# The two seams of the expert stage rewritten: token rows scaled on VectorE, no softmax division, the last expert's rows in two halves, and the last layer norm by sum and square

## The reference

```python
# m = W_o(sum of three gated branches of x); one projection w_in feeds all branches
h = layer_norm(ALPHA * x + m, ln1_g, ln1_b)
# moe_ffn(h)
logits = jnp.dot(t, router_w) + router_b          # t: 520 tokens x 1024
probs = jax.nn.softmax(logits, axis=-1)           # 16 experts in 4 groups of 4
top_v, top_i = lax.top_k(probs.reshape(-1, 4, 4), 2)
best = jnp.argmax(jnp.sum(top_v, axis=-1), axis=-1)      # the best group
weights = sel_v / jnp.sum(sel_v, axis=-1, keepdims=True) # its two experts
for e in range(16):
    u = jax.nn.silu(t @ w_gate[e]) * (t @ w_up[e])       # 1024 -> 512
    out = out + gates[:, e:e + 1] * (u @ w_down[e])      # 512 -> 1024
y = layer_norm(ALPHA * h + out, ln2_g, ln2_b)
```

## Time and profile before

| | |
|---|---|
| median of 3 runs | 1061.76 us (1060.02 to 1062.53) |
| the profiled execution | 1062.88 us |
| its span in the trace | 1060.7 us |
| TensorE busy | 993.2 us, 94% |
| VectorE busy | 805.2 us, 76% |
| ScalarE busy | 472.1 us, 45% |
| GpSimd busy | 360.5 us, 34% |
| TensorE's mean granted clock | 0.974 of full speed |
| DMA traffic | 189.91 MB, 179 GB/s over the span |

### The profile page before, as it was taken

One profiled execution on the slowest core, in us unless ns is written; L12 is line 12 of the kernel. 1 busy time (PEld: TensorE's weight loads), 2 busy tenths in 40 slices (PEclk: granted clock), 3 DMA queues, 4 the chain that ended last, 5 costly groups with the idle time before them and its releaser, 6 DMA issues.

```text
span 1060.7 us, 19425 instructions
## 1 busy us (share of the span) xinstructions
PE 993.2 (94%) x7186; PEld 898.5 (85%) x7186; DVE 805.2 (76%) x993; ACT 472.1 (45%) x657; POOL 360.5 (34%) x268
## 2 busy tenths in 40 slices
PE   7999999999999999999999999986999999999940
PEld 7999999999999998999999999964677777777630
DVE  1498889888899985754345596255998989899968
ACT  4232322323222244234342323254887878787820
POOL 2444434444545761454444544401200000000050
PEclk9999999999999999999999999997999999999975
DMA  7332332323322231333335525377999999999562
GB/s 223 106 100 84 94 96 82 99 83 95 96 83 80 79 100 29 122 94 94 88 95 161 176 79 208 111 287 277 313 390 378 393 380 393 381 389 335 178 211 101
DMA packets 162376, 189.91 MB, mean 179 GB/s; under 512 B 5876, under 2 KB 113396, under 8 KB 162317
## 3 DMA queue, kind: packets, MB, share of 16 engines
q1 hardware_dynamic: 155819, 177.46, 49.4%
q0 software_dynamic: 3008, 10.55, 3.1%
q10 hardware_dynamic: 3505, 1.36, 0.5%
HBM read 178.57 MB, written 11.76 MB: 179 GB/s over the span
## 4 chain that ended last, share of the span: by engine, by line
PE 52%; issue 27%; POOL 13%; DVE 3%; DMA 2%; ACT 2%; POOLq 0%; DVEq 0%; ACTq 0%
PE pr L926 27%; PE pr L1099 14%; POOL w_lo L552 12%; PE work L1099 7%; DMA hs<-h_rows,ids 2%; PE work L1085 1%; POOL y_a L609 1%; PE work L1009 1%; DVE stats L1658 1%; DVE y_a L1656 1%; ACT h_f L780 1%; DVE y_b L1665 1%; PE work L1060 1%; DMA y_b<-y_rows,slot_b 0%; PE pr L1116 0%
## 5 line engine op out<-in xcount | busy, mean ns | idle before, releaser
L552 POOL TENSOR_TENSOR w_lo<-raw,w_hi 128x512 fp32r<-128x512 f32 x208 | 297.7, 1452 | 337.1 <-ACT w_hi L637 337.1
L926 PE MATMUL pr<-x_hi,w_hi 128*128 128x260 f32 x1264 | 254.9, 283 | 0.2 <-POOL w_lo L552 0.2
L926 PE MATMUL pr<-x_hi,w_lo 128*128 128x260 f32 x1264 | 254.8, 283 | 0.0
L926 PE MATMUL pr<-x_lo,w_hi 128*128 128x260 f32 x1264 | 254.3, 283 | 0.0
L641 ACT ACTIVATE ev<-pr 128x520 f32<-128x520 f32 x96 | 58.1, 605 | 376.2 <-PE pr L926 376.2
L926 PEld LDWEIGHTS pr<-x_hi,w_hi 128*128 128x128 f32 x1264 | 194.9, 188 | 0.6 <-POOL w_lo L552 0.4
L926 PEld LDWEIGHTS pr<-x_hi,w_lo 128*128 128x128 f32 x1264 | 194.9, 188 | 0.0
L926 PEld LDWEIGHTS pr<-x_lo,w_hi 128*128 128x128 f32 x1264 | 194.3, 188 | 0.0
L1258 DVE SCALAR_TENSOR_TENSOR work<-b_pad,par,work 128x512 f32<-128x512 f32 x224 | 148.1, 743 | 0.0
L637 ACT ACTIVATE w_hi<-raw 128x512 fp32r<-128x512 f32 x208 | 118.9, 623 | 3.5 <-issue 2.2
L588 POOL DMA_INDIRECT hs<-h_rows,ids x16 | 20.1, 1259 | 256.2 <-DVE ids L1518 215.9
(11 more groups left out here) (290 smaller groups left out, 1693.6 us busy)
## 6 DMA issues: line engine op xcount, KB each, us to landing
raw<-in_w_in_dram SPq DMA_DIRECT2D x80, 512.0 KB, 3.7
w_gate<-in_expert_w_gate_dram SPq DMA_DIRECT2D x16, 2048.0 KB, 14.2
w_up<-in_expert_w_up_dram SPq DMA_DIRECT2D x16, 2048.0 KB, 14.3
w_down<-in_expert_w_down_dram SPq DMA_DIRECT2D x16, 2048.0 KB, 12.8
y_rows<-y_out SPq DMA_DIRECT2D x16, 384.0 KB, 12.2
raw<-in_w_a_out_dram SPq DMA_DIRECT2D x8, 512.0 KB, 3.6
raw<-in_w_c_out_dram SPq DMA_DIRECT2D x8, 512.0 KB, 3.6
raw<-in_w_b_out_dram SPq DMA_DIRECT2D x8, 512.0 KB, 3.7
```

Source lines behind the costliest of these rows:

```text
L552: pool.tensor_tensor(w_lo[:, slot, k], raw[:, slot, k], w_hi[:, slot, k].bitcast(F32), ALU.subtract).then_inc(w_split, 1)
L926: mm = pe.matmul(pr[slot][:, h, 0:HALF], w[:, slot, k, :], x[:, k, h * HALF:(h + 1) * HALF], start=(k == 0 and w is w_hi and x is hi), sto ...
```

## The change

- **Seam in.** The gain of the first norm is multiplied into m by ScalarE right behind each projection (zg_ready), so that the router's weights are not scaled. h_f, diag, its matmuls and h_affine are gone. TensorE transposes m itself, the five blocks between the logits' blocks, and VectorE writes the token rows from PSUM: reciprocal deviation times row, plus the bias row (b_row), which SP loads. SP stores the rows ahead of expert 2's gate and up loads.
- **Router.** Exp's table is loaded by a dummy activation behind the roots. The division by the softmax sum is left out (the weights are renormalised later, and the choice doesn't change with the scale). The second top search and the search over the groups run interleaved (behind waits for all but the newest of VectorE's instructions), and the multiplication of the one-hots by the best group moves to pick_weights.
- **First expert.** keep_busy puts 20 transposes of the identity in front of the first turn and 12 behind it. The first gate product starts on hs_hi alone; in its first chunk the low part of the tokens comes last (lo_waits).
- **Slots.** One find_slots for both experts of a token, after expert 13; order_slots after expert 14.
- **Samples.** The 8 sample tokens are spread over all 128 partitions, 16 partitions a token and 64 elements each (CS = 64): TensorE spreads their slots and weights by one matmul, GpSimd fetches with row numbers of 64 elements, and their mean and variance are summed over partitions by two matmuls with block_mean. Two new constant matrices are made by GpSimd. The gain and bias rows for them come by 16 small DMAs.
- **Last expert.** down_last finishes one half of the columns, then the other. ScalarE copies each half into a buffer of its own (y_last), and issues its store itself. GpSimd waits for these two and the other stores, without SP between. The rows of the second norm are loaded by load_back, ahead of the store of expert 14.
- **Second norm.** summed_up sums the row by accum_out and makes the negative mean; ScalarE squares the centred row with accum_out and takes the root. The samples are handled between blocks 2 and 3.

The semaphores are renamed and regrouped to match. The core of the diff, with the constant matrices, the renamed semaphores and the branch for further passes left out:

```diff
-        sp.dma_start(h_back[0:TS, 4, :], h_rows[TP:T, :]).then_inc(back_in, 16)
...
+        sp.dma_start(sh_back, h_rows[TP:T, :].rearrange("s (c f) -> (s c) f", f=CS)).then_inc(back_in, 16)
+        for i, row in enumerate((ln2_g, ln2_b)):
+            sp.dma_start(ln2_rows[:, i, :], row[0].partition_broadcast(P)).then_inc(ln_in, 16)
+            for s in range(TS):
+                k = P // TS
+                sp.dma_start(sln2[s * k:(s + 1) * k, i, :], row[0].rearrange("(c f) -> c f", f=CS)).then_inc(ln_in, 16)
...
+    sp.dma_start(b_row[:], ln1_b[0].partition_broadcast(P)).then_inc(b_row_in, 16)
...
+    h_out()
     expert_load(first, 2, TURN[2], "gate")
     expert_load(first, 2, TURN[2], "up")
...
+    def fetch_samples(dst, which, landed, table):
+
+        pool.indirect_dma_start(out=dst, out_offset=None, in_=table.rearrange("r (c f) -> (r c) f", f=CS),
+                                in_offset=bass.IndirectOffsetOnAxis(ap=s_idx[:, which:which + 1], axis=0)).then_inc(landed[4], 16)
...
     fetch(y_a, slot_early, y_a_in, y_rows[0:EARLY * C, :])
+    pool.wait_ge(sample_dve, 2)
+    fetch_samples(sy_a, 0, y_a_in, y_rows[0:EARLY * C, :])
...
+        pool.wait_ge(first.stored, 16 * E)
+        pool.wait_ge(first.half_stored, 32)
         fetch(y_b, slot_b, y_b_in, y_rows[0:E * C, :])
+        fetch_samples(sy_b, 2, y_b_in, y_rows[0:E * C, :])
...
+        act.wait_ge(sq_ready, i + 1)
+        act.activation(m[:, i, :], m[:, i, :], ACT.Copy, scale=par[:, i * NROWS + R_L1G:i * NROWS + R_L1G + 1]).then_inc(zg_ready, 1)
...
+    act.wait_ge(tok_std, 2)
+    act.activation(agg[0:1, 0, 1:2], eps_t[0:1, 0:1], ACT.Exp)
+    act.wait_ge(var_logits_mm, 2)
...
+    def last_rows_out(ps, t, q, row0):
+        x = E - 1
+        for h in range(2):
+            cols = slice(h * D // 2, (h + 1) * D // 2)
+            act.wait_ge(ps.done["down"], t * CH + CH + 2 * (h + 1))
+            act.activation(y_last[:, cols], work[0][0:C, h, :], ACT.Copy).then_inc(ps.half_ready, 1)
+            act.wait_ge(ps.half_ready, q * 2 + (h + 1))
+            act.dma_start(y_rows[bass.ds(x * C + row0, C), cols], y_last[:, cols]).then_inc(ps.half_stored, 16)
...
+    def deviation(b):
...
         act.wait_ge(var_ready, b + 1)
...
+        act.activation(pr[0][:], y_a[:, b, :].rearrange("p (h n) -> p h n", h=2), ACT.Square, bias=agg[:, s, 1:2],
+                       accum_out=agg[:, s, 2:3]).then_inc(std2_ready, 1)
+        act.wait_ge(std2_ready, 2 * b + 1)
+        act.activation(agg[:, s, 3:4], agg[:, s, 2:3], ACT.Sqrt, scale=1.0 / D, bias=eps_t[:, 1:2]).then_inc(std2_ready, 1)
...
+    def turn_rows(b):
+        n = P if b < 4 else TS
+        work_wait(pe, f"ht{b}")
+        for k in range(KB):
+            mm = pe.transpose(work[TILE[f"ht{b}"]][0:n, k // 4, k % 4 * P:(k % 4 + 1) * P], m[:, k, b * P:b * P + n], ident[:])
...
+    mm.then_inc(var_logits_mm, 1)
+    pe.wait_ge(zg_ready, KB)
+    turn_rows(0)
+    turn_rows(1)
     logits((2, 3))
...
+    turn_rows(2)
+    logits((4,))
+    turn_rows(3)
+    turn_rows(4)
+    logits((5, 6, 7)).then_inc(var_logits_mm, 1)
...
+    def keep_busy(n):
+
+        for _ in range(n):
+            pe.transpose(pr[0][:, 1, 0:P], ident[:], ident[:])
...
+            if lo_waits and i == 0:
+                for kk in range(k_of):
+                    cols = slice(kk * 512, (kk + 1) * 512)
+                    pe.matmul(out(0), hi[:, kk, :], w_hi_i[:, cols], start=(kk == 0), stop=False)
+                    pe.matmul(out(0), hi[:, kk, :], w_lo_i[:, cols], start=False, stop=False)
+                pe.wait_ge(ps.hs_lo_ready, t + 1)
+                for kk in range(k_of):
+                    mm = pe.matmul(out(0), lo[:, kk, :], w_hi_i[:, kk * 512:(kk + 1) * 512], start=False, stop=False)
+                mm.then_inc(ps.done[kind], 1)
+                continue
...
-        product(ps, "down", 0, t, u_hi_last, u_lo_last, lambda h: work[0][0:C, h, :], 2, last=True)
+        for h in range(2):
+            for k in range(CH):
+                if h == 0:
+                    pe.wait_ge(ps.lo_dve["down"], t * CH + (k + 1))
+                cols = slice(h * 512, (h + 1) * 512)
+                w_lo_k, w_hi_k = chunk("down", 0, k, w_e_lo), rounded("down", k, True)
+                for x, w in ((u_hi_last, w_hi_k), (u_hi_last, w_lo_k), (u_lo_last, w_hi_k)):
+                    mm = pe.matmul(work[0][0:C, h, :], x[:, k, :], w[:, cols], start=(k == 0 and x is u_hi_last and w is w_hi_k),
+                                   stop=(k == CH - 1 and x is u_lo_last))
+            mm.then_inc(ps.done["down"], 2)
...
+        if ps is first:
+            keep_busy(20)
         turn(ps, n0)
+        if ps is first:
+            keep_busy(12)
...
+            if m:
+                pe.wait_ge(ps.hs_lo_ready, t + 1)
+            else:
+                pe.wait_ge(ps.hs_hi_ready, t + 1)
...
+        if ps is first:
+            pe.wait_ge(const_ready, 6)
+            pe.wait_ge(sample_dve, 1)
+            pe.matmul(pr[1][:, 1, 8:13], spread[:], s_own[:], start=True, stop=True).then_inc(sample_mm, 1)
...
+        dve.wait_ge(round_done, DONE[f"ht{b}"])
+        dve.scalar_tensor_tensor(h_tok[b][:].rearrange("p (h t) -> p h t", h=2), work[TILE[f"ht{b}"]][0:n], r_tok[0:n, b:b + 1],
+                                 b_row[0:n, :].rearrange("p (h t) -> p h t", h=2), ALU.mult, ALU.add).then_inc(h_tok_ready, 1)
...
-    step(dve.tensor_reduce(s_sum[:], probs[:], AX.X, ALU.add))
-    step(dve.reciprocal(s_sum[:], s_sum[:]))
-    step(dve.tensor_tensor(probs[:], probs[:], over_e(s_sum), ALU.mult))
...
+    def behind(ins):
+
+        chain.wait(1)
+        do(ins())
...
+    step(dve.tensor_reduce(flat(g_m2), grp(probs), AX.X, ALU.max))
+    do(dve.tensor_tensor(grp(oh2), grp(probs), over4(g_m2), ALU.is_equal))
+    do(dve.tensor_tensor(g_t[:], g_m1[:], g_m2[:], ALU.add))
+    behind(lambda: dve.tensor_tensor(grp(oh2), grp(oh2), c4_of(grp(oh2)), ALU.mult))
+    behind(lambda: dve.tensor_reduce(s_max[:], g_t[:], AX.X, ALU.max))
+    behind(lambda: dve.tensor_reduce(best2, grp(oh2), AX.X, ALU.max))
+    behind(lambda: dve.tensor_tensor(g_best[:], g_t[:], rep(s_max[:], 2, GROUPS), ALU.is_equal))
+    behind(lambda: dve.tensor_tensor(grp(oh2), grp(oh2), over4(g_sum), ALU.is_equal))
+    behind(lambda: dve.tensor_tensor(g_best[:], g_best[:], c4_of(g_best), ALU.mult))
+    behind(lambda: dve.tensor_tensor(t2[:], oh1[:], oh2[:], ALU.add))
+    behind(lambda: dve.tensor_reduce(s_t[:], g_best[:], AX.X, ALU.max))
...
+    step(dve.tensor_tensor(g_best[:], g_best[:], rep(s_t[:], 2, GROUPS), ALU.is_equal))
...
+        for t in (oh1, oh2):
+            do(dve.tensor_tensor(grp(t), grp(t), over4(g_best), ALU.mult))
...
-            if ps is first and m == E - 1:
-                order_slots()
...
+                find_slots()
             if ps is first and m == 14:
-                find_slots(oh2, s_slot2)
+                order_slots()
...
+        if ps is first:
+            spread_samples()
...
+        do(dve.tensor_tensor(t2[:], oh1[:], e_off[:], ALU.mult))
+        step(dve.tensor_tensor(probs[:], oh1[:], pos[:], ALU.mult))
+        step(dve.tensor_tensor(oh1[:], oh2[:], e_off[:], ALU.mult))
+        step(dve.tensor_tensor(oh2[:], oh2[:], pos[:], ALU.mult))
+        do(dve.tensor_reduce(s_pair[:, 0, :], t2[:], AX.X, ALU.add))
+        do(dve.tensor_reduce(s_pos[:, 0, :], probs[:], AX.X, ALU.add))
+        do(dve.tensor_reduce(s_pair[:, 1, :], oh1[:], AX.X, ALU.add))
+        step(dve.tensor_reduce(s_pos[:, 1, :], oh2[:], AX.X, ALU.add))
+        do(dve.tensor_tensor(s_pair[:], s_pair[:], s_pos[:], ALU.add))
+        over = s_over[:].rearrange("p i b k -> p (i b) k")
+        step(dve.tensor_tensor(over, rep(s_pos[:].rearrange("p i b -> p (i b)"), 2, PASSES - 1), rep(kc[:], 1, 2 * NTB), ALU.is_ge))
+        step(dve.tensor_reduce(s_add[:].rearrange("p i b -> p (i b)"), over, AX.X, ALU.add))
+        step(dve.scalar_tensor_tensor(s_pair[:], s_add[:], float(E * C - C), s_pair[:], ALU.mult, ALU.add))
...
+    def spread_samples():
+
+        last[0] = chain
+        dve.wait_ge(sample_mm, 1)
+        step(dve.tensor_copy(s_spread[:], pr[1][:, 1, 8:13]))
+        dve.scalar_tensor_tensor(s_idx[:], s_spread[:, 0:3], float(P // TS), id_cols[:, 0, 1:2].to_broadcast([P, 3]), ALU.mult,
+                                 ALU.add).then_inc(sample_dve, 1)
...
         dve.wait_ge(y_b_in[b], 16)
...
+        step(dve.scalar_tensor_tensor(y_a[:, b, :], y_b[:, b, :], s_wb[:, b:b + 1], y_a[:, b, :], ALU.mult, ALU.add,
+                                      accum_out=agg[:, s, 0:1]))
+        do(dve.tensor_scalar(agg[:, s, 1:2], agg[:, s, 0:1], -1.0 / D, None, ALU.mult), to_var)
...
+        s = b % 2
+        to_var.wait(0 if b == 3 else 1)
+        do(dve.scalar_tensor_tensor(y_b[:, b, :], y_a[:, b, :], agg[:, s, 1:2], ln2_rows[:, 0, :], ALU.add, ALU.mult))
+        dve.wait_ge(std2_ready, 2 * b + 2)
+        do(dve.reciprocal(agg[:, s, 3:4], agg[:, s, 3:4]))
```

(21 more changed lines are left out.)

319 lines of the change are left out of this document (154 added, 165 removed).

## The result

| | before | after |
|---|---|---|
| median | 1060.93 us (4 runs, 1060.02 to 1062.53) | 1047.72 us (4 runs, 1045.03 to 1051.01) |
| the profiled execution | 1062.88 us | 1048.14 us |
| its span | 1060.7 us | 1046.4 us |
| TensorE's mean granted clock | 0.974 | 0.978 |

The ratio is 0.9875 with a 95% interval of 0.9843 to 0.9907: 13.2 us faster, where 13.2 were forecast (1047.72 measured, 1048.6 predicted). A second set of runs gave 1048.32 against 1061.86. The total is right, and some of its terms are not: most of all the one for the seam into the experts.

What follows compares the result with a forecast made beforehand. TensorE, busy 214.74 of 215 us in the expert stage, was taken as the bound, so only its two ends could move: 1.9 + 2.7 + 9.0 - 0.4 = 13.2 us, from 1061.76 to 1048.6; range 1044.5 to 1054.0.

Steps and rivals of the forecast that it cites:

- What bounds the kernel: Expert stage: TensorE busy 214.74 of 215 us at full clock, loop carried over unchanged; only its two ends can move.
- Router, first ids, gather 0, turn 1: Seam in: router at 709.6, ids 0 at 717.9, gather 0 issued at 718.75; gather 1, awaited by turn 1, landing at 734.4.
- Seam in: 1.9 us gained: From router to second expert's turn: 1.9 us gained, bounds 0.3 and 5, limited by gather 1's landing.
- Before the last rows: Experts 13 to 15: less VectorE work removes TensorE's waits of 1.05 and 0.85 us, less 0.25 for a matmul: 1.65 us.
- The store's 0.6: Last copy's end to y_b's fetch: half the bytes stored, 3.5 us instead of 4.14, 0.6 us gained.
- y_b's landing: Seam out, from the fetch of y_b to its landing: claimed to stay at 5.1 us.
- The last store: End of the kernel: 512 KB instead of 32 KB, 2.6 us instead of 2.2, 0.4 us lost.
- The norm: VectorE's last stretch: 26.54 us falls to 17.55, 4.0 a block, row sums at 0.15 each: 9.0 us gained.
- The rival on the summing pass: Second norm: row summing costs two passes, 4.5 us back, 1053.1 us; chance 0.07.
- The table switch: First norm block: Sqrt table load 1.28 us, all but 0.25 hidden; with the skill's 1.38 us drain, the root about 1.6 late.
- Gather 1 was not quick: Rival at the seam in: gather 1 overtakes the loads, seam gives 5 us, time 1045.5; chance 0.12.
- The clock rival: Seam in: clock stays 1.2 GHz despite dummy transposes, gate 0 ends near 735.5, gain 0.9, 1049.6 us; no separate chance.

Runs made afterwards that it cites:

- e4_downs_later: Changed kernel with the down loads of experts 1 and 2 issued after the second gather's landing, not the first's: 1045.76 us, ratio 0.9842 to the kernel before.
- e2: Changed kernel without the 20 and 12 dummy transposes around the first turn: 1047.69 us, ratio 0.9857 to the kernel before.
- e3: Changed kernel with 26 more dummy transposes in front of the second turn: 1045.94 us, ratio 0.9845 to the kernel before.
- e7: Changed kernel with the last expert's rows copied in one operation and stored by one 384 KB DMA: 1048.80 us, ratio 0.9883 to the kernel before.
- e8: Changed kernel with the prompt blocks' statistics by bn_stats and bn_aggr on VectorE again, no Square on ScalarE: 1053.82 us, ratio 0.9914 to the kernel before.
- e1_again: Changed kernel run once more without any edit, as baseline: 1048.32 us, ratio 0.9861 to the kernel before.
- e12: Changed kernel with only expert 2's down load issued after the second gather's landing: 1046.10 us, ratio 0.9852 to the kernel before.
- e9: Changed kernel with expert 1's down load ahead of the h stores and expert 2's after the second gather's landing: 1048.22 us, ratio 0.9876.
- e10: Changed kernel with expert 1's down load ahead of the h stores, expert 2's still after the first gather's landing: 1048.71 us, ratio 0.9871.
- e5: Changed kernel with a second gathered-rows buffer, the second gather issued right behind the first: 1048.86 us, ratio 0.9872 to the kernel before.
- e6: Changed kernel with the last expert's two half stores issued by SP, not ScalarE: 1047.53 us, ratio 0.9857 to the kernel before.
- e11: Changed kernel with order_slots back between the second and third up chunks of expert 15: 1049.66 us, ratio 0.9882 to the kernel before.

## Why the prediction was right, and where it was not

- **What bounds the kernel.** "Nothing in the change touches that loop, so it is carried over": true for this change, but the row that has TensorE busy at full clock also has the DMA engines full (share 1.04, 383 GB/s), which the prediction did not read. e4_downs_later shows how thin the lead is.
- **Router, first ids, gather 0, turn 1**: right within 0.4 us each.
- **"Seam in: 1.9 us gained"** is the step that failed. Its way to turn 1 was right, 2.1 us earlier. The 3 us of idle before turn 1 were forecast too, and the clock that follows such an idle was in hand and even a rival for gate 0, but it was not carried to what stands behind the new idle: turn 1 and up 0 were put at nothing. They cost 2.8 us (10.30 from turn to gate 1 against 7.50), so the change lost 0.67 here. The runs in which the clock did not fall give the sum back: 2.4 us gained at gate 1 in e2, 1.7 in e3 and 2.0 in e7, near the forecast.
- **Before the last rows**: 1.65 us for the waits was too little; 2.54 came, and 1.3 to 2.8 in the other profiles (e4 apart). The waits alone are 1.90, and turn 3 had waited 0.26 for its gather (769.77); the rest was not isolated. Copy 0.43 as worked out. The store's 0.6 came in this profile. That it comes from half the bytes is not shown (e7), and the signal by way of SP, which also went, was not tested by itself.
- **y_b's landing** was kept at 5.1 and is 4.4 to 4.8 in every run: 0.5 us not counted, cause open.
- **The last store** was put at 0.4 us more, 2.6 against 2.2, and took 0.85 more. The 2.6 run from a store's issue to its landing, the 2.2 from VectorE's last operation to the end of the span. Measured alike it is 3.05 against 2.2.
- **The norm**: 9.20 for 9.0; 3.99 and 4.18 us from block to block, the second with a short operation of the samples in it. Of the sum's 0.15 a block 0.08 came, and the root was ready before VectorE wanted it (1030.37 against 1030.55), not 0.25 late. e8 gives the size of the statistics' part, 4.7 us.
- **The rival on the summing pass** was argued from a wrong comparison. The Trainium skill (Vector Engine (DVE) Microarchitecture Reference, Points that are easy to get wrong) has this operation at half the throughput with two fp32 sources. The prediction set against it that it is as fast as a plain one, but the plain ones of that length in SBUF, the subtractions for the low parts at 1.22 us, have two sources as well. An operation of the same 128x1024 with one source, the TENSOR_SCALAR on wo at L1398, takes 0.75 us before (median of eight), against 1.28: that bears the page out. What did not come is a further loss by the sum: 1.28 us with it and without.
- **The table switch.** The drain that the same skill adds (ScalarE: Activation LUTs, What ACT_TABLE_LOAD costs) did not show: Sqrt began 1.30 us after the load did.
- **Rivals.** GpSimd was done at 1014.7, 2.7 us before the last copy; its first fetch of y_a took 7.43 us, but 24 us ahead of y_b. Gather 1 was not quick (8.2). SP's 20 issues took 10.7 us, 0.54 each. The clock rival was placed at the wrong product, gate 0 and not up 0.
- The gain of 13.2 us fits because the 2.6 us missed at the seam and 0.45 at the last store are made up by 0.9 in the experts, 0.5 at y_b, 0.2 in the norm and the 1.4 us without a place. That is luck in good part.

The best versions, e3 and e4, stand at 0.9845 and 0.9842 against 0.9861 for e1_again. The intervals overlap, so the times do not show that either beats the changed kernel. In the traces the two stretches together are 2.8 us shorter than in e1_again for e3, 1.4 for e4 and 1.7 for e12.

## What to carry to other kernels

Where a change makes an engine wait at a new place, price what runs behind the wait at the clock that the trace shows after such a wait, and follow the saved time until the next resource that is already full. Dummy work that keeps the clock up is worth placing only in front of a product that nothing later waits out; in front of one behind which the engine waits for a transfer anyhow, it bought nothing here (e2). When terms are read from one pair of profiles, count both from a point behind the first loads.

## What the runs showed of the hardware

- A gather of 96 rows of 4 KB (gather 1) landed in 4.2 to 4.3 us when no 2 MB load had been issued in the 10 us before it (e4, e9), in 7.4 and 8.2 us behind one (e12, e10) and in 8.2 to 9.5 us behind two (nine profiles, the one of before among them). Issued 2.4 us behind another gather it held GpSimd for 4.50 us and landed in 11.9 (e5). A load under way is not enough by itself to slow a gather so much: gather 0 of e1_again was issued at 718.73, with expert 2's up load landing at 721.6 and the DMA engines at 389 GB/s, and took 4.2 us. How much is left of the loads seems to count, which no run isolates.
- After 2.98, 3.44, 3.66, 3.37 and 3.18 us of idle ahead of turn 1 (after, e1, e6, e8, e11), and after 2.17 in e12, TensorE came back at 1.2 GHz. After 3.04 us in e7 it stayed at 2.4 GHz. After 1.92 us in e5 the granted clock was 0.96 up to 734 us and 0.50 from there to 736, so it fell about 0.7 us after turn 1 had begun (733.29). So in this seam the length of the idle alone does not tell whether the clock falls.
- Half a store (192 KB) took 2.9 to 4.2 us from the end of its copy to the fetch in eleven profiles (4.74 in e11), the whole (384 KB) 3.78 in e7 and 4.14 before.
- VectorE's SCALAR_TENSOR_TENSOR on 128x1024 fp32 took 1.28 us with accum_out and without, plus 0.08 us for the read of the sum.
